# Final RMSNorm of an encoder: statistics with tokens on partitions, rstd spread by transposition, results shared by two engines

## The reference

```python
def rms_norm(x, g):
    xf = x.astype(jnp.float32)
    y = xf * lax.rsqrt(jnp.mean(xf * xf, axis=-1, keepdims=True) + EPS)
    return (y * g.astype(jnp.float32)).astype(x.dtype)

def squared_relu_mlp(h, w_in, w_out):
    u = jnp.square(jax.nn.relu(jnp.einsum('bsd,df->bsf', h, w_in)))
    return jnp.einsum('bsf,fd->bsd', u, w_out)

def reference(x, ...):
    for i in range(DEPTH):
        ...
        h = rms_norm(x, mlp_norm[i])
        x = x + squared_relu_mlp(h, mlp_w_in[i], mlp_w_out[i])
    return rms_norm(x, final_norm)
```

## Time and profile before

| | us |
|---|---|
| median of 3 runs | 1175.71 |
| lowest, highest | 1175.38, 1176.13 |
| the profiled execution | 1175.7 |
| its span, first to last instruction | 1174.0 |
| PE, DVE, ACT, POOL busy | 98%, 53%, 40%, 11% of the span |

### The profile page before, as it was taken

One profiled execution on the slowest core, in us unless ns is written; L12 is line 12 of the kernel. 1 busy time (PEld: TensorE's weight loads), 2 busy tenths in 40 slices (PEclk: granted clock), 3 DMA queues, 4 the chain that ended last, 5 costly groups with the idle time before them and its releaser, 6 DMA issues.

```text
span 1174.0 us, 16835 instructions
## 1 busy us (share of the span) xinstructions
PE 1150.0 (98%) x5770; PEld 949.1 (81%) x5770; DVE 623.4 (53%) x988; ACT 466.4 (40%) x811; POOL 129.6 (11%) x243
## 2 busy tenths in 40 slices
PE   6999999999999999999999999999999999999996
PEld 4788888877888888888888788887888888888886
DVE  7676666575443324444345788766544233454335
ACT  6445545344342213433223666644443122443221
POOL 4734332050000000000000122100000000000000
PEclk9999999999999999999999999999999999999998
DMA  7422221142223223232232122122222323223222
GB/s 199 119 70 83 67 85 54 56 133 94 104 89 106 92 91 106 89 103 85 98 107 90 51 63 63 34 71 90 104 93 90 107 89 104 92 90 106 90 89 90
DMA packets 36850, 106.74 MB, mean 91 GB/s; under 512 B 8224, under 2 KB 10544, under 8 KB 36816
## 3 DMA queue, kind: packets, MB, share of 16 engines
q1 hardware_dynamic: 31680, 98.98, 25.2%
q0 software_dynamic: 4992, 7.29, 2.8%
q10 hardware_dynamic: 144, 0.02, 0.0%
HBM read 102.92 MB, written 3.34 MB: 91 GB/s over the span
## 4 chain that ended last, share of the span: by engine, by line
PE 91%; DVE 3%; issue 1%; POOL 1%; ACT 1%; SPq 1%; DMA 1%; DVEq 0%; ACTq 0%; POOLq 0%
PE acc L364 26%; PE acc L366 25%; PE acc L365 25%; PE s_ps L436 3%; PE o_ps L469 2%; PE o_ps L466 2%; PE pt_ps L626 1%; PE pt_ps L457 1%; DVE w_lo L967 1%; SPq L262 1%; PE misc_ps L469 1%; PE misc_ps L426 1%; POOL bias_pairs L292 1%; PE s_ps L364 1%; PE misc_ps L466 1%
## 5 line engine op out<-in xcount | busy, mean ns | idle before, releaser
L721 ACT CAST w_hi<-w_raw 128x1024 fp32r<-128x1024 f32 x180 | 188.8, 1049 | 416.4 <-PE acc L366 412.5
L364 PE MATMUL acc<-h_hi,w_hi 128*128 128x512 f32 x800 | 324.4, 406 | 10.3 <-DVE sqsum L984 9.8
L366 PE MATMUL acc<-h_hi,w_lo 128*128 128x512 f32 x800 | 313.4, 392 | 0.0
L365 PE MATMUL acc<-h_lo,w_hi 128*128 128x512 f32 x800 | 313.0, 391 | 0.0
L967 DVE TENSOR_TENSOR w_lo<-w_raw,w_hi 128x1024 fp32r<-128x1024 f32 x180 | 221.4, 1230 | 153.1 <-ACT w_hi L721 153.0
L364 PE MATMUL acc<-u_hi,w_hi 128*128 128x512 f32 (+1 forms) x624 | 241.4, 387 | 0.9 <-DVE w_lo L967 0.9
L366 PE MATMUL acc<-u_hi,w_lo 128*128 128x512 f32 (+1 forms) x624 | 239.5, 384 | 0.0
L365 PE MATMUL acc<-u_lo,w_hi 128*128 128x512 f32 (+1 forms) x624 | 239.4, 384 | 0.0
L364 PEld LDWEIGHTS acc<-h_hi,w_hi 128*128 128x128 f32 x800 | 150.9, 189 | 48.6 <-issue 14.2
L366 PEld LDWEIGHTS acc<-h_hi,w_lo 128*128 128x128 f32 x800 | 150.9, 189 | 32.4
L365 PEld LDWEIGHTS acc<-h_lo,w_hi 128*128 128x128 f32 x800 | 151.4, 189 | 29.0 <-issue 1.2
(11 more groups left out here) (105 smaller groups left out, 989.1 us busy)
## 6 DMA issues: line engine op xcount, KB each, us to landing
w_raw<-in_wstream SPq DMA_DIRECT2D x180, 512.0 KB, 3.3
bias_pairs<-rpb_shifted POOLq DMA_DIRECT2D x64, 48.0 KB, 3.0
bias_pairs<-t_shifted POOLq DMA_DIRECT2D x64, 48.0 KB, 2.1
x_res<-in_xT SPq DMA_DIRECT2D x8, 256.0 KB, 4.6
out_y<-x_res SPq DMA_DIRECT2D x16, 128.0 KB, 1.8
t_shifted<-vT POOLq DMA_DIRECT2D x16, 31.0 KB, 2.0
rpb_shifted<-rpb_pad SPq DMA_DIRECT2D x8, 45.0 KB, 8.5
rpb_shifted<-rpb_pad POOLq DMA_DIRECT2D x8, 45.0 KB, 5.3
```

The source lines that it names most:

```text
L364: nc.tensor.matmul(dst, a[0], b[0], start=start, stop=False)
L365: nc.tensor.matmul(dst, a[0], b[1], start=False, stop=False)
L366: return nc.tensor.matmul(dst, a[1], b[0], start=False, stop=stop)
L721: nc.scalar.copy(w_hi[:, c.odd, :], w_raw[:, c.odd, :]).then_inc(w_hi_made, 1)
```

## The change

1. Statistics: instead of ones as weights and squares as the moving operand, the squares (128 tokens at a time) are the weights and one column of ones moves. The sum then stands with tokens on partitions, as one column for each 128 tokens, two columns for each half. Four such products replace the two of L569, two replace each one of L577.
2. Root and reciprocal work on two columns, in the new tile `last_std`.
3. `spread_rstd(n)`: PE transposes each column, broadcast over 128 columns, into PSUM. This gives rstd again on all partitions, 256 tokens wide. For the first half it stands ahead of block 10 of the second half's products, for the second half at the end, where a second pair of transposes makes a copy in another bank for ACT.
4. DVE's results read rstd from PSUM.
5. Of the second half's eight results, tiles 4, 5 and 6 are made by GpSimd. ACT multiplies them by the gain beforehand and copies rstd from PSUM to SBUF for it; GpSimd multiplies, and ACT's own DMA queue stores them. DVE makes the other five and SP stores these.

```diff
+Y_BY_DVE, Y_BY_POOL = [0, 1, 2, 3, 7], [4, 5, 6]
...
-        last_stats = [misc_ps[:].rearrange("p a b -> p (a b)")[:, 0:SEQ // 2],
-                      pt_ps[:, 0:2, :].rearrange("p a b -> p (a b)")]
+        last_stats = [[misc_ps[:, 0, 0:1], o_ps[:, 0, 0:1]], [pt_ps[:, 0, 0:1], s_ps[:, 0, 0:1]]]
+        last_rstd = [misc_ps[:, 2:4, :], pt_ps[:, 2:4, :]]
+        rstd_for_act = s_ps[:, 1, 0:SEQ // 2].rearrange("p (b n) -> p b n", b=2)
...
@block.sync
+            for n, k in enumerate(Y_BY_DVE):
+                sp.wait_ge(y_made, KT + n + 1)
+                sp.dma_start(out[k][:, half_tokens[1]], x[:, k, half_tokens[1]]).then_inc(y_stored, 16)
...
@block.gpsimd
+            t = half_tokens[1]
+            pool.wait_ge(x_scaled, len(Y_BY_POOL))
+            pool.wait_ge(last_rstd_copied, 1)
+            for k in Y_BY_POOL:
+                nc.gpsimd.tensor_tensor(x[:, k, t], x[:, k, t], rstd[:, t], ALU.mult).then_inc(y_made_by_pool, 1)
...
@block.tensor, last_group
                             if n == 1 and kk == 5:
                                 last_statistics(0)
+                            if n == 1 and kk == 10:
+                                spread_rstd(0)
...
-                            for h, t2 in enumerate(half_tokens):
-                                nc.tensor.matmul(last_stats[h], ones[:], sqsum[:, t2], start=True, stop=False)
+                            for h in range(2):
+                                for b in range(2):
+                                    nc.tensor.matmul(last_stats[h][b], sqsum[:, (2 * h + b) * P:(2 * h + b + 1) * P],
+                                                     ones[:, 0:1], start=True, stop=False)
...
                 last_statistics(1)
+                spread_rstd(1)
...
-                nc.tensor.matmul(last_stats[n], ones[:], last_square[:, t], start=False,
-                                 stop=True).then_inc(stat_done, 1)
+                for b in range(2):
+                    ins = nc.tensor.matmul(last_stats[n][b], last_square[:, (2 * n + b) * P:(2 * n + b + 1) * P],
+                                           ones[:, 0:1], start=False, stop=True)
+                ins.then_inc(stat_done, 1)
+
+            def spread_rstd(n):
+
+                pe.wait_ge(rstd_made, NORMS + n)
+                for b in range(2):
+                    ins = nc.tensor.transpose(last_rstd[n][:, b, :], last_std[:, n, b:b + 1].to_broadcast([P, P]), ident[:])
+                ins.then_inc(last_rstd_done, 1)
+                if n == 1:
+                    for b in range(2):
+                        ins = nc.tensor.transpose(rstd_for_act[:, b, :], last_std[:, n, b:b + 1].to_broadcast([P, P]), ident[:])
+                    ins.then_inc(last_rstd_done, 1)
...
@block.scalar, last_squares
-                    nc.scalar.activation(rstd[:, t], last_stats[n], ACT.Sqrt, bias=eps[:], scale=1.0 / D
-                                         ).then_inc(std_made, 1)
+                    for b in range(2):
+                        ins = nc.scalar.activation(last_std[:, n, b:b + 1], last_stats[n][b], ACT.Sqrt, bias=eps[:],
+                                                   scale=1.0 / D)
+                    ins.then_inc(std_made, 1)
+                    if n == 0:
+                        act.wait_ge(x_prepared, KT * NORMS - 1)
+                        for k in Y_BY_POOL:
+                            late = half_tokens[1]
+                            nc.scalar.activation(x[:, k, late], x[:, k, late], ACT.Copy,
+                                                 scale=gain[:, 4 * KT + k:4 * KT + k + 1]).then_inc(x_scaled, 1)
+                act.wait_ge(last_rstd_done, 3)
+                nc.scalar.copy(rstd[:, half_tokens[1]], flat(rstd_for_act)).then_inc(last_rstd_copied, 1)
+                for n, k in enumerate(Y_BY_POOL):
+                    act.wait_ge(y_made_by_pool, n + 1)
+                    act.dma_start(out[k][:, half_tokens[1]], x[:, k, half_tokens[1]]).then_inc(y_stored_by_act, 16)
...
@block.vector, last_norm
-                    nc.vector.reciprocal(rstd[:, t], rstd[:, t]).then_inc(rstd_made, 1)
-                    dve.wait_ge(rstd_made, NORMS + n)
+                    nc.vector.reciprocal(last_std[:, n, :], last_std[:, n, :]).then_inc(rstd_made, 1)
+                    dve.wait_ge(last_rstd_done, n + 1)
...
-                                                   scalar=gain[:, 4 * KT + k:4 * KT + k + 1], in1=rstd[:, t],
+                                                   scalar=gain[:, 4 * KT + k:4 * KT + k + 1], in1=flat(last_rstd[n]),
...
-                for k in range(KT):
+                for k in Y_BY_DVE:
                     result(1, k)
```

More of the change, by code:

```diff
@@ L140, in encoder @@
         t5_row = vT[0:HEADS, :]
+        last_std = sb("last_std", [P, 2, 2])
         sw_sink, sw_nsink = sb("sw_sink", [P, 2, 2]), sb("sw_nsink", [P, 2, 2])
@@ L182, in encoder @@
         y_made = sem("y_made")
+        last_rstd_done, x_scaled = sem("last_rstd_done"), sem("x_scaled")
+        last_rstd_copied, y_made_by_pool, y_stored_by_act = sem("last_rstd_copied"), sem("y_made_by_pool"), sem("y_stored_by_act")
         half_tokens = [slice(0, SEQ // 2), slice(SEQ // 2, SEQ)]
-        last_stats = [misc_ps[:].rearrange("p a b -> p (a b)")[:, 0:SEQ // 2],
-                      pt_ps[:, 0:2, :].rearrange("p a b -> p (a b)")]
+        last_stats = [[misc_ps[:, 0, 0:1], o_ps[:, 0, 0:1]], [pt_ps[:, 0, 0:1], s_ps[:, 0, 0:1]]]
+        last_rstd = [misc_ps[:, 2:4, :], pt_ps[:, 2:4, :]]
+        rstd_for_act = s_ps[:, 1, 0:SEQ // 2].rearrange("p (b n) -> p b n", b=2)
         LAST_G = GR_MLP1 + 24 + HALF + KT - 1
@@ L266, in _ @@
                     load_weights(At(n, 2, i))
-            for n, t in enumerate(half_tokens):
-                for k in range(KT):
-                    sp.wait_ge(y_made, KT * n + k + 1)
-                    sp.dma_start(out[k][:, t], x[:, k, t]).then_inc(y_stored, 16)
-            sp.wait_ge(y_stored, 16 * 2 * KT)
+            for k in range(KT):
+                sp.wait_ge(y_made, k + 1)
+                sp.dma_start(out[k][:, half_tokens[0]], x[:, k, half_tokens[0]]).then_inc(y_stored, 16)
+            for n, k in enumerate(Y_BY_DVE):
+                sp.wait_ge(y_made, KT + n + 1)
+                sp.dma_start(out[k][:, half_tokens[1]], x[:, k, half_tokens[1]]).then_inc(y_stored, 16)
+            sp.wait_ge(y_stored, 16 * (KT + len(Y_BY_DVE)))
+            sp.wait_ge(y_stored_by_act, 16 * len(Y_BY_POOL))
         @block.gpsimd
@@ L567, in last_group @@
                             pe.wait_ge(h_split, KT * NORMS - 1)
-                            for h, t2 in enumerate(half_tokens):
-                                nc.tensor.matmul(last_stats[h], ones[:], sqsum[:, t2], start=True, stop=False)
+                            for h in range(2):
+                                for b in range(2):
+                                    nc.tensor.matmul(last_stats[h][b], sqsum[:, (2 * h + b) * P:(2 * h + b + 1) * P],
+                                                     ones[:, 0:1], start=True, stop=False)
                     ins.then_inc(w_used, 1)
                 last_statistics(1)
+                spread_rstd(1)
             def last_statistics(n):
-                t = half_tokens[n]
                 pe.wait_ge(x_prepared, KT * NORMS + n)
-                nc.tensor.matmul(last_stats[n], ones[:], last_square[:, t], start=False,
-                                 stop=True).then_inc(stat_done, 1)
+                for b in range(2):
[11 more added lines that the diff above has]
+                    ins.then_inc(last_rstd_done, 1)
             def mlp(ch, gr, ti, norm):
```

## The result

The changed kernel takes 1182.46 us (median of 5 runs, 1182.32 to 1182.79), the kernel before 1175.71 (5 runs): a ratio of 1.0064, 95% interval 1.0052 to 1.0075. It is slower by 6.75 us; the forecast was faster by 1.7. Its profiled execution has a span of 1180.8 where before had 1174.0.

The account below looks back on a forecast made before the run. TensorE, busy 98%, bounds the kernel, so only the tail counts: first second-half result 1.04 us earlier, two store queues near full DMA share, span 1172.3, plus 1.7 around it: 1174.0 us, a gain of 1.7; range 1173.2 to 1175.2.

Parts of the forecast that it names:

- last group on PE lengthened: Two transposes added ahead of block 10 of 16 in the second half's products cost PE 0.22 us.
- PE set the second addition: First-half results end at 1163.7, before PE, so PE releases the second half's addition to x, 0.22 us later.
- signs of being wrong: PE standing still ahead of block 10, a one-column fp32 pass over 0.2, or a table load between scaling and root.
- the hand-over: Passing the rstd copy out of PSUM on to GpSimd before its products: about 0.05 us.
- Rival 1: Store phase: DMA engines are the bound, so it only shifts by 1.04 us, giving 1174.65 us; chance 0.15.
- Rival 2: Second-half results: DVE and GpSimd exclude each other, DVE ends at 1171.15, giving 1175.1 us; chance 0.12.
- Rival 3: GpSimd's three products: slow after long idleness, last result slips 2.5 us, giving 1176.2 us; chance 0.05.
- the last term: End of the span: 2.2 us after the last issue at 1169.76, or 0.8 after the data's end.
- the way by the data: Store end: first data at 1168.1, 3.2 to 3.85 us for eight tiles, plus 0.8, giving 1172.1 to 1172.8.
- the stated range: Kernel time from 1173.2 to 1175.2 us, taking in all but rival 3 and some of rival 2's far side.
- allowed 0.4: Second half's transposes near 1166.5: up to 0.4 us more if the granted clock falls to half.

Follow-up runs that it names:

- early-drain kernel: The changed kernel plus one explicit drain on GpSimd behind its last bias load, some 420 us before its three products: 1172.93 us, ratio 0.9986.
- mark on GpSimd: The kernel before, plus GpSimd waiting for the first second-half result and filling one column nobody reads: 1180.97 us, ratio 1.0047.
- half of the DMAs: The changed kernel plus one GpSimd drain at about 200 us, behind 76 of its 156 software DMAs, leaving 80: 1177.68 us, ratio 1.0027.
- drain behind the first 28: The changed kernel plus one GpSimd drain at 40 us, behind 28 of its 156 software DMAs, leaving 128: 1184.09 us, a single run.

## Why the prediction was wrong

Step by step, counted from the start of the last dense product (us; the forecast put it at 1163.90, measured 1164.16):

| step | forecast | measured |
|---|---|---|
| last group on PE lengthened | 0.22 | 0.22 |
| second addition starts | 0.31 | 0.32 |
| statistics take | 0.58 | 0.62 |
| two roots of one column | 0.42 | 0.42 |
| reciprocal ends | 2.49 | 2.51 |
| first second-half result | 3.02 | 3.03 |
| DVE's five end | 5.10 | 5.08 |
| GpSimd starts | 3.66 | 3.77 |
| GpSimd's three end | 5.80 | 5.86 |
| last issue | 5.86 | 5.89 |
| end of the span | 8.40 | 16.64 |

- **Right, up to the last issue.** PE set the second addition; the reciprocal fell to 0.17; the first result came 1.25 earlier than before by this clock (3.03 against 4.28). PE's group grew by 0.22 (12.83 to 13.05 from 1150.85 and 1151.11); the last dense product starts 0.48 later, the other 0.26 is from further up. None of its signs of being wrong came: PE didn't stand still ahead of block 10, a one-column pass cost 0.62 / 4 = 0.16, and no table load stands between ScalarE's scaling and the root. The only steps off by more than 0.05 are GpSimd's start, since the hand-over takes 0.14 and not 0.05, and its end, by 0.06.
- **Rival 1, DMA engines as the bound at 273 GB/s: refuted.** With two queues they move 322 to 348 GB/s at a share of 0.96 to 1.02. But its thought holds one level up: at that rate they seem to be the bound (the kernel with two results by GpSimd speaks for it). The Trainium skill ("DMA: Bandwidth & Descriptors", Issuing engines are not separate DMA queues) says that a second issuer saves only issue time, usually small beside the transfer. The trace agrees that the engines are shared, but the saving wasn't small here: at 0.47 an issue on SP it was 0.66 of the tail, more than GpSimd's results.
- **Rival 2, DVE stalling beside GpSimd: refuted for this form.** Five results in 2.05, 0.39 apart. It shows once rstd is read from SBUF.
- **Rival 3, GpSimd late: the right engine and the wrong reason.** Its products took 0.72, 0.69 and 0.68 and its start cost nothing. The prediction gave it until 1171.8 before it would be slower than before, and asked only about its work. Its DRAIN was put at nothing.
- **The step that failed** is the last term: "with the 2.2 us from last issue to end" and "plus 0.8" from the end of the data. Both were read from an execution in which GpSimd had closed 416 us before, and were used for one in which GpSimd closes last. The wait for GpSimd's closing DRAIN was put at nothing, without a reason, and it measured 10.6. The right term is the later of two ends: the data's end plus 0.8 = 1171.85 + 0.8 = 1172.65 (SP's closing step began at 1172.6, and in the kernel before it stands 0.2 ahead of the end), and GpSimd's last product plus 10.6 = 1170.02 + 10.6 = 1180.6. The 11.0 was in the trace of before, at 746.5, on a line that the busy times leave out.

With that term out of the way the rest of the sum is nearly right: the early-drain kernel has a tail of 8.60 where the forecast had 8.40. It is the way by the data (full share, plus 0.8) that comes near; from the last issue to the end it took 8.60 - 5.89 = 2.7 and not 2.2. Its ratio of 0.9986 makes 1174.1 of 1175.71, beside the forecast of 1174.0. Its median by itself, 1172.93, lies 0.3 below the stated range. That the closing drain is the cause is shown from four sides: the mark on GpSimd alone brings the loss to the kernel before, the early drain and the missing one both take it away, and half of the DMAs bring half of it.

## What to carry to other kernels

Before an engine that finished early gets work near the end, look in the trace at the instructions that close each engine's stream: their cost is hidden only as long as nothing is placed ahead of them. If that engine has issued software DMAs, count 0.08 to 0.09 us for each since its last drain (here of 32 packets each), 10.6 us at most here, and put a drain of its own where nobody waits for it, or leave the engine out of the tail. Here leaving it out costs nothing: a second queue for the stores and DVE for all results give the same tail within what one execution tells; that the DMA engines are then the limit is likely, by their full share, but no kernel here varied it alone.

## What else the runs showed of the hardware

**The granted clock falls soon after dense work ends, not always at the same distance.** It is 0.50 from about 1167.5 in the kernel before, 3.5 us after the end of the last dense product; about 4 us after it in the changed kernel; but from about 1165.05, 2.1 us after it, in the kernel without the closing drain, and from 1168.0, 2.4 us after it, in the kernel with the drain behind the first 28. In these two the transposes fell into it. In the kernel with the mark on GpSimd it fell as late as 4.8 us after. First that kernel's timeline, then the changed one's:

```profile
1165.23 0.69 PE L604 MATMUL pt_ps<-ident,last_std 128*128 128x128 f32 x2 [0.70 <-DVE last_std L1190]
```
```profile
1166.72 0.43 PE L604 MATMUL pt_ps<-ident,last_std 128*128 128x128 f32 x2 [0.70 <-DVE last_std L1190]
```

The pair takes 0.69 instead of 0.43 (0.64 with the drain behind the first 28), and the first result comes 0.25 later (3.28 behind the last dense product instead of 3.03). The prediction had allowed 0.4 for this. A tail of small fp32 products behind dense work has this scatter in it, and why the distance differs no run here shows.

**A long idle GpSimd starts at its full pace.** After 420 us without work its first product took 0.72, the next 0.69 and 0.68, and from the end of ACT's copy to its start were 0.14. The slow first copy of the earlier trace rows, 0.58 where 0.20 is usual, did not come back.
